# A two-layer float32 model on one core: the order of loads, splits and transposes at its start

## The reference

```python
def rms_norm(x, g):
    y = x * lax.rsqrt(jnp.mean(x * x, axis=-1, keepdims=True) + EPS)
    return y * g

h = x
for layer in range(2):
    hn = rms_norm(h, norm_mix[layer])
    if layer == 0:     # windowed attention and a gated recurrence, side by side
        proj = hn @ w_in                       # 2048 x 3584
        h = h + concat(attention(q, k, v), rg_lru(xb, gb)) @ w_out
    else:              # stick-breaking attention, 16 heads of 128
        h = h + stick_breaking(hn @ w_in) @ w_out
    hn = rms_norm(h, norm_mlp[layer])
    h = h + jnp.square(jax.nn.relu(hn @ w_up[layer])) @ w_down[layer]
return rms_norm(h, final_norm)
```

## Time and profile before

| | us |
|---|---|
| median of 3 runs | 2101.09 |
| lowest and highest | 2100.72, 2101.97 |
| the profiled execution | 2100.86 |
| its span in the profile | 2099.1 |
| PE busy | 2083.3 |
| DVE busy | 1243.8 |
| ACT busy | 1029.2 |

### The profile page before, as it was taken

The page is one execution under the profiler, slowest core; times in us unless marked ns, Lnnn a source line. Parts: engine busy times, 40 slices in busy tenths (PEclk is TensorE's granted clock), DMA queues, the critical chain, the costliest instruction groups (busy, mean ns, idle before and its releaser), DMA issues.

```text
span 2099.1 us, 29916 instructions
## 1 busy us (share of the span) xinstructions
PE 2083.3 (99%) x10819; PEld 1767.9 (84%) x10819; DVE 1243.8 (59%) x1579; ACT 1029.2 (49%) x1429; POOL 40.7 (2%) x81
## 2 busy tenths in 40 slices
PE   8999999999999999999999999999999999999998
PEld 7887888888888888888888888888888888888886
DVE  6798556555655655655545666566546546645654
ACT  6588555434434444544444444455434434534454
POOL 3010000000000000000000000000000000000000
PEclk9999999999999999999999999999999999999999
DMA  8544656666566666665665554656665666666664
GB/s 263 172 142 150 208 183 189 191 194 189 189 194 192 185 197 184 188 195 187 189 191 179 162 161 151 203 184 192 193 191 183 197 192 189 186 195 189 192 191 148
DMA packets 297967, 390.96 MB, mean 186 GB/s; under 512 B 12273, under 2 KB 205457, under 8 KB 297745
## 3 DMA queue, kind: packets, MB, share of 16 engines
q1 hardware_dynamic: 296656, 385.72, 59.0%
q0 software_dynamic: 944, 3.70, 0.6%
q10 hardware_dynamic: 272, 0.29, 0.0%
HBM read 387.53 MB, written 2.12 MB: 186 GB/s over the span
## 4 chain that ended last, share of the span: by engine, by line
PE 99%; ACT 0%; DMA 0%; DVE 0%; issue 0%; SPq 0%; DVEq 0%
PE psum L397 50%; PE psum L422 15%; PE psum L424 15%; PE psum L423 15%; PE psum L456 1%; PE psum L1053 0%; PE psum L1209 0%; PE psum L1251 0%; DMA h<-in_x_dram 0%; PE psum L1237 0%; PE psum L1208 0%; PE psum L995 0%; PE psum L585 0%; PE psum L583 0%; PE psum L584 0%; PE psum L1253 0%
## 5 line engine op out<-in xcount | busy, mean ns | idle before, releaser
L376 DVE TENSOR_TENSOR w_split<-raw,w_split 128x1024 fp32r<-128x1024 f32 x728 | 888.2, 1226 | 767.7 <-ACT w_split L369 766.4
L369 ACT ACTIVATE w_split<-raw 128x1024 fp32r<-128x1024 f32 x728 | 766.9, 1058 | 860.1 <-PE psum L424 491.2
L397 PE MATMUL psum<-hg_op,w_split 128*128 128x512 f32 (+1 forms) x6016 | 1067.8, 338 | 0.0
L397 PEld LDWEIGHTS psum<-hg_op,w_split 128*128 128x128 f32 x6016 | 917.4, 188 | 136.2 <-issue 2.9
L422 PE MATMUL psum<-w_split,ff_op 128*128 128x512 f32 x1264 | 493.4, 390 | 1.1 <-DVE w_split L376 1.1
L424 PE MATMUL psum<-w_split,ff_op 128*128 128x512 f32 x1264 | 491.9, 389 | 0.0
L423 PE MATMUL psum<-w_split,ff_op 128*128 128x512 f32 x1264 | 491.8, 389 | 0.0
L422 PEld LDWEIGHTS psum<-w_split,ff_op 128*128 128x128 f32 x1264 | 237.3, 188 | 49.8 <-DVE w_split L376 1.5
L424 PEld LDWEIGHTS psum<-w_split,ff_op 128*128 128x128 f32 x1264 | 237.2, 188 | 49.7
L423 PEld LDWEIGHTS psum<-w_split,ff_op 128*128 128x128 f32 x1264 | 237.3, 188 | 48.8
L437 ACT ACTIVATE cross<-psum 128x256 f32<-128x256 f32 x188 | 66.1, 380 | 56.0 <-PE psum L397 55.9
(11 more groups left out here) (158 smaller groups left out, 583.0 us busy)
## 6 DMA issues: line engine op xcount, KB each, us to landing
raw<-in_w_up_dram SPq DMA_DIRECT2D x256, 512.0 KB, 3.8
raw<-in_w_down_dram SPq DMA_DIRECT2D x256, 512.0 KB, 3.8
raw<-in_odd_w_in_dram SPq DMA_DIRECT2D x96, 512.0 KB, 3.7
raw<-in_even_w_in_dram SPq DMA_DIRECT2D x56, 512.0 KB, 4.2
raw<-in_even_w_out_dram SPq DMA_DIRECT2D x32, 512.0 KB, 4.5
raw<-in_odd_w_out_dram SPq DMA_DIRECT2D x32, 512.0 KB, 3.7
early_r<-rel_dram POOLq DMA_DIRECT2D x4, 512.0 KB, 5.7
h<-in_x_dram SPq DMA_DIRECT2D x3, 512.0 KB, 8.6
```

What stands on the lines that cost most here:

```text
L369: act.activation(w_hi[:, slot], raw[:, rs], ACT.Copy).then_inc(hi_done, 1)
L376: dve.tensor_tensor(w_lo[:, slot], raw[:, rs], w_hi[:, slot].bitcast(F32), ALU.subtract).then_inc(lo_done, 1)
L397: ins = nc.tensor.matmul(o, l, r, start=(k == 0 and n == 0), stop=(k == KT - 1 and n == 1), skip_group_check=True)
```

## The change

SP's list of loads is ordered anew. The first weight piece is loaded, split and multiplied in two halves of two k tiles each, with signals of their own (`raw_first`, `hi_first`, `lo_first`). x2 is issued behind w1 (the second piece), x3 and x4 behind w2 and ahead of w3. PE transposes pairs 2 and 3 behind P0 instead of ahead of it, pairs 4 and 5 behind P2 instead of P0, pairs 6 and 7 behind P4 instead of P1; ACT and DVE follow with their parts, and the sums of squares move behind them. The norm's factor is made one place later. PE makes six products of a matrix of ones, which nobody reads, as its first work, and six more just ahead of P0. The norm vectors of the first layer are the first load in both.

```diff
+        def pe_sub_first(pe, op):
+            for half in range(2):
+                pe.wait_ge(lo_done if half else lo_first, 1)
+                pe.wait_ge(hg_ready, 2 * half + 2)
+                for j in range(2):
+                    for k in (2 * half, 2 * half + 1):
...
+                            ins = nc.tensor.matmul(o, l, r, start=(k == 0 and n == 0), stop=False, skip_group_check=True)
+            ins.then_inc(pe_count, 1)
...
         def norm_hook(n):
-            place = 5 if n == 0 else 3
+            place = 6 if n == 0 else 3
...
         def start_sync(sp):
             sp.dma_start(prow[0:32, 0], norm_mix.rearrange("l (t p) -> (l t) p", p=P)).then_inc(norm_in, 16)
-            for c, (a, b) in enumerate(X_COLS):
-                sp.dma_start(h[:, :, a:b], x[0, :, a:b].rearrange("(b p) d -> p b d", p=P)).then_inc(x_in[c], 16)
-                if c:
-                    load_quad(sp, 0, w_even_in, 0, EVEN_IN_COLS[0], False, (c - 1,))
+            x_piece(0)
+            first_half(0, 0)
+            x_piece(1)
+            first_half(2 * P, 2)
+            for place, pieces in ((1, (2,)), (2, (3, 4)), (3, ())):
+                load_quad(sp, 0, w_even_in, 0, EVEN_IN_COLS[0], False, (place,))
+                for c in pieces:
+                    x_piece(c)
...
+        def unused_pe(pe, count):
+            for _ in range(count):
+                nc.tensor.matmul(psum[:, 7, 0:P], ones[:], ones[:], start=True, stop=True)
+
         def start_pe(pe):
+            pe.wait_ge(const_done, 1)
+            unused_pe(pe, 6)
...
-            x_pe_pair(pe, 2)
-            x_pe_pair(pe, 3)
             pe.wait_ge(par_done, 1)
+            unused_pe(pe, 6)
...
         def start_act(act):
-            x_act_hi(act, 0)
-            x_act_hi(act, 1)
-            split_hi(act, 0, 0 - AHEAD)
+            for half in range(2):
+                x_act_hi(act, half)
+                split_first(act, half)
             split_hi(act, 0, 1 - AHEAD)
             x_act_square(act, 0)
             x_act_square(act, 1)
-            x_act_pair(act, 2)
-            x_act_pair(act, 3)
+            x_act_hi(act, 2)
+            x_act_hi(act, 3)
             split_hi(act, 0, 2 - AHEAD)
...
-        for m, k in ((4, 0), (5, 0), (6, 1), (7, 1)):
+        for m in range(2, 8):
+            k = 2 * (m // 2) - 2
             at_key("pe", k, x_pe_pair, m)
-        for m in range(4, 8):
-            at_key("act", m - 4, x_act_pair, m)
-            at_key("dve", m - 4, x_dve_lo, m)
+            if m >= 4:
+                at_key("act", k + 1, x_act_hi, m)
+                at_key("dve", k + 1, x_dve_lo, m)
+        for m, k in ((2, 0), (3, 0), (4, 3), (5, 3), (6, 4), (7, 4)):
+            at_key("act", k, x_act_square, m)
```

More of the change, by code:

```diff
@@ L226, in build @@
         raw_in = [sem(f"raw_in{i}") for i in range(RAW_SLOTS)]
+        raw_first, hi_first, lo_first = sem("raw_first"), sem("hi_first"), sem("lo_first")
         hi_done = sem("hi_done")
@@ L376, in split_lo, with split_first, lo_of_first @@
             dve.tensor_tensor(w_lo[:, slot], raw[:, rs], w_hi[:, slot].bitcast(F32), ALU.subtract).then_inc(lo_done, 1)
+        def pe_sub_first(pe, op):
[4 more added lines that the diff above has]
+                    for k in (2 * half, 2 * half + 1):
+                        hi = (psum[:, j, 0:2 * S], w_hi[:, 0, k, j * P:(j + 1) * P], op[:, k, :])
+                        lo = (psum[:, j, 0:S], w_lo[:, 0, k, j * P:(j + 1) * P], op[:, k, 0:S])
+                        for n, (o, l, r) in enumerate((hi, lo) if k % 2 == 0 else (lo, hi)):
+                            ins = nc.tensor.matmul(o, l, r, start=(k == 0 and n == 0), stop=False, skip_group_check=True)
+            ins.then_inc(pe_count, 1)
+        def split_first(act, half):
+            act.wait_ge(raw_in[0] if half else raw_first, 16)
+            kt = slice(2 * half, 2 * half + 2)
+            act.activation(w_hi[:, 0, kt], raw[:, 0, kt], ACT.Copy).then_inc(hi_done if half else hi_first, 1)
+        def lo_of_first(dve, half):
+            dve.wait_ge(hi_done if half else hi_first, 1)
+            kt = slice(2 * half, 2 * half + 2)
+            dve.tensor_tensor(w_lo[:, 0, kt], raw[:, 0, kt], w_hi[:, 0, kt].bitcast(F32),
+                              ALU.subtract).then_inc(lo_done if half else lo_first, 1)
         def pe_sub(pe, Q, s, pos, op, ready, base, first, after_wide):
@@ L558, in quad_pe @@
             for place, s in enumerate(order(Q)):
-                pe_sub(pe, Q, s, place, op, ready, base, s < 4, after_wide)
+                if isinstance(Q, int) and Q == 0 and place == 0:
+                    pe_sub_first(pe, op)
+                else:
+                    pe_sub(pe, Q, s, place, op, ready, base, s < 4, after_wide)
                 if hook:
@@ L651, in norm_hook @@
         def norm_hook(n):
-            place = 5 if n == 0 else 3
+            place = 6 if n == 0 else 3
             def hook(which, eng, s):
-                if which == "dve" and s == place - 2:
+                if which == "dve" and s == (place - 1 if n == 0 else place - 2):
                     norm_sum(eng, n)
@@ L675, in start_sync, with x_piece, first_half @@
         def start_sync(sp):
-            sp.dma_start(prow[0:32, 0], norm_mix.rearrange("l (t p) -> (l t) p", p=P)).then_inc(norm_in, 16)
-            for c, (a, b) in enumerate(X_COLS):
-                sp.dma_start(h[:, :, a:b], x[0, :, a:b].rearrange("(b p) d -> p b d", p=P)).then_inc(x_in[c], 16)
-                if c:
-                    load_quad(sp, 0, w_even_in, 0, EVEN_IN_COLS[0], False, (c - 1,))
+            def x_piece(c):
+                a, b = X_COLS[c]
+                sp.dma_start(h[:, :, a:b], x[0, :, a:b].rearrange("(b p) d -> p b d", p=P)).then_inc(x_in[c], 16)
+            def first_half(rows, n):
+                src = w_even_in[bass.ds(rows, 2 * P), bass.ds(EVEN_IN_COLS[0], GC)]
+                sp.dma_start(raw[:, 0, n:n + 2], src.rearrange("(t p) n -> p t n", p=P)).then_inc(
+                    raw_in[0] if n else raw_first, 16)
+            sp.dma_start(prow[0:32, 0], norm_mix.rearrange("l (t p) -> (l t) p", p=P)).then_inc(norm_in, 16)
+            x_piece(0)
[6 more added lines that the diff above has]
+                    x_piece(c)
             sp.dma_start(prow[C_W:C_W + 4 * NL, 1], even_conv_w[0].rearrange("w (t p) -> (w t) p", p=P)).then_inc(lru_in, 16)
@@ L779, in x_act_square @@
             square_act(act, 0, m // 2, m % 2)
-        def x_act_pair(act, m):
-            x_act_hi(act, m)
-            x_act_square(act, m)
         def x_dve_lo(dve, m):
@@ L805, in start_dve @@
             dve.wait_ge(par_done, 1)
-            x_dve_lo(dve, 0)
-            x_dve_lo(dve, 1)
-            split_lo(dve, 0, 0 - AHEAD)
+            for half in range(2):
+                x_dve_lo(dve, half)
+                lo_of_first(dve, half)
             dve.wait_ge(par_pe, 2)
```

## The result

The changed kernel takes 2104.86 us (median of 20 runs, 2103.98 to 2107.01), the kernel before 2101.33 in the same measurement (2099.82 to 2102.79). The ratio is 1.0019, 95% interval 1.0013 to 1.0025: 3.5 us slower. I had forecast 2102.5, which is 1.4 above the median of 2101.09 then known, and a range up to 2104.8; the time stands 0.06 above its upper end. One run of one experiment (e13) took 3385.62 us at a mean granted clock of 0.574, where every other run here stands at 0.997 to 0.999; it has no trace and is left out of the comparison.

What follows compares the result with a forecast made beforehand. PE bounds the kernel, busy 2083.3 of 2099.1 us. P6 later by 0 to 0.4 (P4's start) + 0.87 (owed transposes) + 0.3 (wait), taken as 1.4, on the median 2101.09 gives 2102.5 us; range 2099.5 to 2104.8.

Steps and rivals of the forecast that it cites:

- What bounds it, and where the waits come: Whole kernel: PE bounds it, most of its 15.8 idle us ahead of 9.70; new waits at P2, P4 and P6.
- P0 at 10.56 (10.0 to 10.8): Start of P0: x1's transposes from 7.5, unused block from 8.5, so P0 starts at 10.0 to 10.8.
- P0: First weight piece: slow level ends inside the unused block, P0 takes 2.80 us, P1 stands at 14.5 to 15.3.
- rival B: Start: array stays slow to between 12.5 and 14.1, P0 starts at 11.1, +2.4 to +3.2 us; chance 0.18.
- P4, the wait that decides: P4 waits for pairs 4 and 5, by w6 or w5; starts at 25.6 to 26.0, PE waiting 1.4 to 1.9 us.
- rival D: Ahead of P4: w6 lands late, at 6.9 instead of 3.9 us in flight, +4.4 us; chance 0.06.
- P6: Behind P4: P8's parts, norm's sum, pairs 6 and 7 take 7.5 us against PE's 7.2; PE waits 0.3.
- The gain of the start does not enter: the waits take it all: Sum at P6: an earlier P1, 1.0 to 1.8 us gained, does not count towards the time.
- second way to P4, by w5: P4's wait: w5 lands at 20.4, then high part 1.05 and low parts on DVE, giving 25.5.
- The rule on the clock: Start: activity lifts the slow level; forecast ends it at about 10.7, the trace's unmoved moment of 14.1 gives rival B's time.
- Rival C: Streams of ACT and DVE: splits run ahead, P4 hardly waits, -0.8 to -1.8 us, 2099.3 to 2100.3; chance 0.22.

Runs made afterwards that it cites:

- e13: e9 with POOL's loads of gate weights and bias moved behind the last part of x: 2099.00 us, 1.9 below the kernel before, ratio 0.9990.
- e3: Changed kernel with POOL's loads of gate weights and bias made to wait for the last part of x: 2104.93 us, 3.9 above the kernel before.
- e12: Changed kernel with twelve instead of six unused products ahead of P0: 2106.62 us, 5.3 above the kernel before.
- e11: Changed kernel without any unused products: 2102.89 us, 1.5 above the kernel before.
- e10: Changed kernel with the loads of x2, x3 and x4 back in their old places: 2104.93 us, 3.6 above the kernel before.
- e1: Changed kernel without the six unused products just ahead of P0, the first six kept: 2102.90 us, 1.9 above the kernel before.
- e6: e3 with ten more unused products behind P3, where PE waits for pairs 4 and 5: 2104.23 us, 3.2 above the kernel before.
- e4: Kernel before, with POOL's loads of gate weights and bias made to wait for the last part of x: 2100.84 us, 0.2 below the kernel before.
- e14: e7 with POOL's loads moved behind the last part of x: 2099.77 us, 1.1 below the kernel before.
- e8: e5 with three unused products between the transposes of x0 and x1 and three ahead of P0: 2102.28 us, 1.2 above the kernel before.
- e7: Kernel before with only unused products added (six first, one between x0 and x1, four ahead of pairs 2 and 3): 2099.87 us, 1.2 below the kernel before.
- e2: Changed kernel with pairs 4 and 5 transposed behind P1, pairs 6 and 7 behind P2: 2104.16 us, 3.1 above the kernel before.
- e5: e2 without the second unused block, sums of squares and the norm's sum one place further forward: 2102.71 us, 1.7 above the kernel before.
- e9: e8 with DVE's sum for the norm one more place forward, ahead of P7's low part: 2102.22 us, 0.9 above the kernel before.

## Why the prediction was wrong, step by step

**What bounds it, and where the waits come: right, with one wrong reading.** Waits came at P2, P4 and P6, each released as forecast, and nothing was made up behind P6. That most of PE's 15.8 idle us lie ahead of 9.70 was wrong: 6.9 do, and 7.9 lie in the last 10 us. Nothing hangs on it.

**P0 at 10.56 (10.0 to 10.8): the number by luck.** x1's transposes came at 6.7, not 7.5, so the block began at 8.0, not 8.5; and all of it was slow, 2.6 us, where I let the slow level end inside it. The two errors cancel.

**"P0": the end of the slow level was mis-sized.** I let it end inside the block, at about 10.7; the products are slow to 12.8, so P0's own products last to 14.46, where a fast P0 would have ended at 13.4. That is rival B's condition (slow to between 12.5 and 14.1), without its P0 start of 11.1. P2 started at 18.93, not 17.3 to 18.1: this 1.1 us. From P0 to P2 the way itself was right, 8.4 us with the 1.1 in it, against 7.3.

**"P4, the wait that decides": the landing of w6 was mis-sized.** I took its 3.9 us from the earlier trace rows, and had the "nearly empty" queue as the reason against rival D. Measured 5.2, and in e3, issued at 16.2, 7.1. Over the traces of all these kernels w6 was issued between 15.7 and 19.4 and landed between 21.6 and 24.1: issuing it early brings it little. P4 came at 28.1, not 25.6 to 26.0; of these 2.3 us 1.3 are the transfer and the rest is P2's.

**"P6": w8's landing was mis-sized, and in this profile it is the one that decided.** I took 28.6 "anyway"; it landed at 31.7, issued 0.4 later and with 9.5 us in flight instead of 6.8. ACT can write P8's high part once P4 is through and once w8 is there, and all that P6 needs stands behind it. The seven profiles with pairs 6 and 7 in this place show it, P6 starting 4.6 to 4.8 us behind the later of the two (the figures are starts plus durations, in us):

| run | P4 ends | w8 lands | P6 starts |
|---|---|---|---|
| changed kernel | 31.2 | 31.7 | 36.5 |
| e12 | 30.1 | 32.7 | 37.4 |
| e11 | 28.7 | 29.6 | 34.2 |
| e10 | 30.2 | 29.7 | 34.9 |
| e1 | 30.5 | 28.9 | 35.2 |
| e6 | 30.6 | 26.6 | 35.3 |
| e3 | 32.7 | 26.2 | 37.4 |

I had both at about 28.7, and P6 at 33.2 to 33.6. Both came late. By this table w6 in time alone would have brought nothing, and w8 in time alone 0.6 us. In e3 and e6, which bring w8 in after 4.5 us, P4 had the say, and so the time was not won back.

POOL's loads of the gate weights and the bias are the reason for w8's length: with them moved back (e3, e4, e6, e13, e14) w8 took 4.2 to 4.9, and with them in their old place 4.7 (e8) to 10.0 (e12).

Together: P6 at 36.5, not 33.2 to 33.6. The median is 1 us closer to the forecast than this one profile, 3.5 against 4.5.

**The second block has no price in the sum.** By "The gain of the start does not enter: the waits take it all", six products more or less ahead of P0 should change nothing; e1 and e12 show 1.7 us each time, where six slow ones take 2.6 and six fast ones 1.3. P0's end leads through ACT and DVE to the issue of w6 and of w8 (the chain above). My second way to P4, by w5, bound in no trace: in e1 and e11, which start earlier, the chain goes back to w3, which landed at 17.2 and 16.7, and from there by the high and low parts of P4 to P6.

**The rule on the clock.** The trace of before has its last slow product at 14.1, the changed kernel at 12.8, e7 at 10.0. The Trainium skill, "TensorE: Matmul & The Clock Gate", Part 1, says that the slow level is the default and that the moment of release moves from run to run. The traces agree: e2, e3 and e6 have PE's work up to P0 in common with the changed kernel, and P0 took 3.91, 3.04 and 4.15 there against 4.06. So my time for the end of the slow level could only have been a guess, and so could the unmoved one.

**Rival C** was never seen in the changed kernel. **B** comes nearest, by its condition and by its time (+2.4 to +3.2). **D** as priced, a 6.9 for w6, was not reached, but its mechanism, a load that lands later than its row said, is there twice. The range went to B's 2104.3 and 0.5 beyond, though the highest run then shown stood 0.9 above the median.

Open: why w6 takes 5.2 us in the changed kernel, where w5 had landed 0.8 us behind its issue (with POOL's loads out of the way it took 4.8 in e6 and 3.6 in e4); how often the array goes slow behind a wait; and what the halves of the first piece are worth, since no run took them out.

## What to carry to other kernels

A piece of work that is moved back in an in-order stream comes to depend on every load ahead of it; list these loads, and take for each the longest flight among its neighbours, not its own from one trace. Where two things must both have come, price both: mending the one that is not the later gains nothing (e3, e12). When a wait is removed, look for the next one in the same stream before expecting a gain: here it took pairs, sum and POOL's loads together (e2, e5, e9, e13) until the start's gain came through. Unused products helped only in gaps that PE had anyway (e7 and e14, 1.2 and 1.1 us, each with an interval that holds 1), and six ahead of ready work cost 1.7 us (e1, e12).

## What I had not expected of the hardware

TensorE goes back to the slow level behind a wait of a few us in the middle of dense work, and the length of the wait does not tell whether. In the profiles it did behind waits of 4.4 us (e3), 3.5 (e9), 2.3 (e8), 2.0 (e1) and 1.8 (e5), and did not behind 3.2 (e2), 2.5 (changed kernel) and 2.4 (e10), where the pieces behind it took as long as ever. In e3 that cost P4 2.3 us on top of the wait, in e1 1.5.
